# Two transformer blocks on one core: the grouped-query mixer's attention and output projection in another order, and a weight split moved in each FFN

## The reference

```python
def odd_mixer(x, mix_norm, w_qkv, q_norm, k_norm, w_out):
    proj = rms_norm_2(x, mix_norm) @ w_qkv                  # 1024 -> 1536
    q, k, v = jnp.split(proj, [GQA_Q_WIDTH, GQA_Q_WIDTH + GQA_KV_WIDTH], axis=-1)
    q = rms_norm_2(q.reshape(Bsz, S, 16, 64), q_norm)       # 16 heads
    k = rms_norm_2(k.reshape(Bsz, S, 4, 64), k_norm)        # 4 key/value heads
    q, k = apply_rope(q, cos, sin), apply_rope(k, cos, sin)
    return gqa_block_attention(q, k, v) @ w_out             # softmax over 256 keys

def swiglu_ffn_2(x, norm_g, w13, w2):
    g, u = jnp.split(rms_norm_2(x, norm_g) @ w13, 2, axis=-1)
    return (jax.nn.silu(g) * u) @ w2
...
x = x + odd_mixer(...)
x = x + swiglu_ffn_2(...)
```

## Time and profile before

| | |
|---|---|
| median of 3 runs | 1721.07 us (1718.12 to 1721.99) |
| the profiled execution | 1720.91 us |
| its span in the trace | 1719.6 us |
| mean granted TensorE clock | 0.982 |
| TensorE busy | 1641.7 us, 95% of the span |
| VectorE busy | 974.2 us, 57% |
| ScalarE busy | 786.2 us, 46% |
| the odd stage, first projection matmul to first gate matmul of f | 1407.0 to 1528.5 us |

### The profile page before, as it was taken

The page is one execution under the profiler, slowest core; times in us unless marked ns, Lnnn a source line. Parts: engine busy times, 40 slices in busy tenths (PEclk is TensorE's granted clock), DMA queues, the critical chain, the costliest instruction groups (busy, mean ns, idle before and its releaser), DMA issues. The chain is left out here.

```text
span 1719.6 us, 18632 instructions
## 1 busy us (share of the span) xinstructions
PE 1641.7 (95%) x7938; PEld 1343.2 (78%) x7938; DVE 974.2 (57%) x992; ACT 786.2 (46%) x954; POOL 68.4 (4%) x99
## 2 busy tenths in 40 slices
PE   6999998999999999998999999998999997699999
PEld 5877876788888888797788879876788885488887
DVE  4655675545455545645645466877554467545543
ACT  4535444444444443544544446745434345534341
POOL 1000000100000000100100010100000012000000
PEclk9999998999999999999999999999999999799999
DMA  8545542355545554541654544424545443035451
GB/s 328 194 160 185 188 154 85 126 223 190 193 172 202 192 190 177 202 184 57 237 186 181 196 160 195 148 88 109 208 172 196 171 175 147 1 125 218 172 196 50
DMA packets 51391, 289.33 MB, mean 168 GB/s; under 512 B 14151, under 2 KB 14791, under 8 KB 18026
## 3 DMA queue, kind: packets, MB, share of 16 engines
q1 hardware_dynamic: 50732, 286.84, 45.8%
q10 hardware_dynamic: 576, 1.29, 0.2%
HBM read 287.06 MB, written 1.05 MB: 168 GB/s over the span
## 5 line engine op out<-in xcount | busy, mean ns | idle before, releaser
L1764 DVE TENSOR_TENSOR wl<-raw,wh 128x2048 fp32r<-128x2048 f32 x260 | 588.9, 2287 | 156.3 <-ACT wh L1150 156.3
L516 PE MATMUL ps<-wh,xTh 128*128 128x512 f32 x1408 | 558.1, 396 | 20.3 <-DVE wl L1764 8.3
L516 PE MATMUL ps<-wh,xTl 128*128 128x512 f32 x1408 | 552.0, 392 | 0.0
L516 PE MATMUL ps<-wl,xTh 128*128 128x512 f32 x1408 | 551.3, 392 | 0.0
L1150 ACT ACTIVATE wh<-raw 128x2048 fp32r<-128x2048 f32 x260 | 488.9, 1908 | 3.8 <-PE ps L516 2.6
L516 PEld LDWEIGHTS ps<-wh,xTh 128*128 128x128 f32 x1408 | 266.3, 189 | 85.3 <-DVE xTl L1803 10.6
L516 PEld LDWEIGHTS ps<-wh,xTl 128*128 128x128 f32 x1408 | 266.0, 189 | 56.6
L516 PEld LDWEIGHTS ps<-wl,xTh 128*128 128x128 f32 x1408 | 266.4, 189 | 53.7
L2456 POOL TENSOR_SCALAR st<-st 128x1 f32<-128x1 f32 (+2 forms) x46 | 29.5, 640 | 1463.2 <-ACT tmp L1169 850.6
L1213 ACT ACTIVATE sgf<-ps,st 128x256 f32<-128x256 f32 x22 | 10.5, 476 | 104.2 <-PE ps L516 104.2
L1213 ACT ACTIVATE sge<-ps,st 128x256 f32<-128x256 f32 x22 | 10.5, 476 | 98.9 <-PE ps L516 98.9
(11 more groups left out here) (330 smaller groups left out, 2260.8 us busy)
## 6 DMA issues: line engine op xcount, KB each, us to landing
raw<-in_w SPq DMA_DIRECT2D x260, 1024.0 KB, 4.8
gains<-in_rows SPq DMA_DIRECT2D x18, 512.0 KB, 4.1
x<-in_x ACTq DMA_DIRECT2D x2, 512.0 KB, 8.6
nab<-in_rpb SPq DMA_DIRECT2D x32, 32.0 KB, 2.6
out_x<-x SPq DMA_DIRECT2D x2, 512.0 KB, 2.6
qn<-in_rpb SPq DMA_DIRECT2D x16, 32.0 KB, 2.5
xd<-in_rpb SPq DMA_DIRECT2D x16, 32.0 KB, 2.5
df<-in_cst SPq DMA_DIRECT2D x1, 368.0 KB, 23.4
```

Of the source, the lines that this page charges most:

```text
L516: return pe.matmul(o, lhs, rhs, start=start, stop=stop, skip_group_check=False)
L1764: TT(wl[:, p % RAW, :], raw[:, p % RAW, :], wh[:, p % RING, :].bitcast(F32), ALU.subtract).then_inc(*lo(p))
```

## The change

It has two parts.

**1. The odd stage is written in another order**, with its own programs on TensorE, ScalarE and VectorE in place of the shared `attention` and `close`.

- TensorE: q's second half is done in quarters of 6 matmuls (`q_quarter(t, n)`), put between the first scores and turns. From pair 2 on, `out(i, t)`, 6 matmuls of the output projection for one pair and tile, stand between a pair's attention steps: per iteration `scores(i + 1)`, `out(i - 3, 1)`, `values(i - 1)`, `turn(i, 0)`, `out(i - 2, 0)`, `turn(i, 1)`. Both turns of a pair use bank 6 (pair 7: banks 4 and 5), values bank 7, all scores banks 4 and 5. f's tile 0 is turned between the two halves of the very last `out(7, 1)`, with 3 matmuls behind it.
- q is no longer scaled by its norm. VectorE rotates it straight from PSUM; the squares go to a tile of their own (`qsq`); GpSimd writes the roots to a table (`gqa_root`), ScalarE's exponential takes them as its scale, and VectorE multiplies the negated maxima by them (one 128 x 2 multiplication a head). The four 128 x 512 scalings of q are gone.
- ScalarE and VectorE handle a pair head by head, not tile by tile. A dummy exponential at the stage's start loads the table there.
- ScalarE and VectorE copy the turned tile 1 earlier in their programs: VectorE ahead of the tables of gains and of all work on k, ScalarE ahead of `vg`. The splits of the stage's later pieces are spread one an iteration, ahead of the exponentials on ScalarE.

**2. `ring.fill(1, p0)` ahead of the turned input is taken away in every FFN**, on ScalarE and on VectorE. Where that call had split a piece, the next `ring.fill` now does.

No matmul, transpose, exponential or weight piece is added or taken away, and the arithmetic is the same but for the place of q's norm.

```diff
@@ tensor_program, odd @@
-                kv_part(0)
-                q_part(0, 0, 5, lambda: turn_in("oddmix", 1))
-                kv_part(1)
-                q_part(0, 1, 1)
-                q_part(1, 0, 4, lambda: [kv_turn(t) for t in range(2)])
-                for t in range(2):
-                    q_turn(0, t)
...
-                attention("gqa", "odd", 8, 64, [256, 256], q_of, k_of, v_of,
-                          {0: lambda: q_part(1, 1, 7), 3: lambda: [q_turn(1, t) for t in range(2)]})
-                close("odd", "ogqa", 8, None)
+                kv_part(0)
+                q_part(0, lambda: turn_in("oddmix", 1))
+                kv_part(1)
+                q_part(1)
+                q_quarter(0, 0)
+                q_quarter(0, 1)
+                kv_turn(0)
+                kv_turn(1)
+                q_turn(0, 0)
+                q_turn(0, 1)
+                q_quarter(0, 2)
+                scores(0)
...
+                for i in range(3, 7):
+                    scores(i + 1)
+                    out(i - 3, 1)
+                    values(i - 1)
+                    turn(i, 0)
+                    out(i - 2, 0)
+                    turn(i, 1)
...
+                out(6, 1)
+                out(7, 1, lambda: turn_in(AFTER["odd"], 0))
@@ scalar_program and vector_program, ffn @@
                 gate(0, 0)
-                ring.fill(1, p0)
                 ring.need(p0 + 4)
                 turn_in(name, 1, free=free)
@@ scalar_program, odd @@
+                turn(2, 0)
+                ring.fill(1, p0 + 3)
+                for i in range(3, 7):
+                    turn(i - 1, 1)
+                    ring.fill(1, p0 + i + 1)
+                    scores(i + 1)
+                    values(i - 1)
+                    turn(i, 0)
@@ vector_program, odd @@
+                def scores(i):
+                    on.wait_ge(scored, "gqa", i)
+                    for hh in range(2):
+                        a = 12 * (i % 3) + 6 * hh
+                        dve.tensor_reduce(r.sm[:, a:a + 2], bank(4 + hh).rearrange("p (t n) -> p t n", t=2), AX.X, ALU.max, negate=True).then_inc(*made("peak", i, hh))
...
+                        TT(r.sm[:, a:a + 2], r.sm[:, a:a + 2], gqa_root(2 * i + hh), ALU.mult).then_inc(*peaked("gqa", i, hh))
...
+                scores(3)
+                ring.fill(1, p0 + 3)
+                values(1)
+                for i in range(3, 7):
+                    scale(i)
+                    scores(i + 1)
+                    ring.fill(1, p0 + i + 1)
+                    values(i - 1)
```

More of the change, by code:

```diff
@@ new lines, in out @@
+                def out(i, t, mid=None):
+                    p, k = p0 + 6 + i // 2, i % 2
+                    on.wait_ge(act_lo, "ogqa", i)
+                    on.wait_ge(*split_of(p))
+                    if i == 0:
+                        clear(2 * t, 2 * t + 1)
+                    H, L = hi_part(p, 2), lo_part(p, 2)
+                    for half in range(2):
+                        if half and mid:
+                            mid()
+                        u = slice(512 * half, 512 * half + 512)
+                        m = mm3(bank(2 * t + half), xTh[:, i, t, :], xTl[:, i, t, :], H[:, k, u], L[:, k, u], i == 0, i == 7)
+                    if t == 1 and k == 1:
+                        m.then_inc(*multiplied(p))
+                    elif i == 7:
+                        m.then_inc(*tail("odd"))
+                    if i == 7:
+                        emptied[2 * t] = emptied[2 * t + 1] = [post_step("odd", t)]
@@ L1726, in odd @@
-                ring.fill(1, p0 + 4)
+                q_stat(0, 1)
+                v_copy(1)
                 ring.need(p0 + 6)
-                for t in range(2):
-                    on.wait_ge(flipped, "kg", t)
-                    act.activation(od.kTg[:, :, 128 * t:128 * t + 128], halves(6 + t), ACT.Copy).then_inc(*copied("kTg", t))
-                q_stat(1, 0, 4)
-                for t in range(2):
-                    q_turn(0, t)
-                def q_turns():
-                    for t in range(2):
-                        q_turn(1, t)
@@ L1739, in odd @@
-                attention("gqa", "odd", 8, 64, [256, 256], xTh, (multiplied, p0 + 5), lambda i: p0 + (6 if i else 4),
-                          {1: lambda: q_stat(1, 1, 7), 3: q_turns})
-                close("odd")
+                k_copy(0)
+                k_copy(1)
+                q_turn(0, 0)
+                q_turn(0, 1)
+                ring.fill(1, p0 + 2)
+                scores(0)
+                q_stat(1, 0)
+                scores(1)
+                turn(0, 0)
+                q_stat(1, 1)
@@ new lines, in odd @@
+                turn(0, 1)
+                turn(1, 0)
+                scores(2)
+                q_turn(1, 0)
+                values(0)
+                turn(1, 1)
+                scores(3)
+                q_turn(1, 1)
+                values(1)
+                turn(2, 0)
+                ring.fill(1, p0 + 3)
[5 more added lines that the diff above has]
+                    turn(i, 0)
@@ L1743, in scalar_program @@
+                turn(6, 1)
+                ring.fill(1, p0 + 8)
+                values(6)
+                turn(7, 0)
+                turn(7, 1)
+                values(7)
+                seam("odd", 0, p0 + 8)
+                turn_in(AFTER["odd"], 0, free=(tail, "odd"))
+                ring.fill(1, p0 + 9)
+                seam("odd", 1, p0 + 10)
             norm_stat("pre00", None, 0)
@@ L2433, in odd @@
-                close("odd")
+                k_rope(1)
+                q_rope(0, 1)
+                ring.need(p0 + 6)
+                q_sum(0, 1)
+                scores(0)
+                ring.fill(1, p0 + 2)
+                scale(0)
+                scores(1)
+                q_rope(1, 0)
+                q_sum(1, 0)
+                scale(1)
+                scores(2)
+                q_rope(1, 1)
+                values(0)
+                q_sum(1, 1)
+                scale(2)
+                scores(3)
```

266 lines of the change are left out of this document (197 added, 69 removed).

## The result

The changed kernel takes **1695.12 us** (median of 4 runs, 1693.43 to 1696.34) against 1721.04 before (1718.12 to 1721.99): ratio 0.9851, 95% interval 0.9837 to 0.9864. The forecast was 1693.8. The profiled execution has a span of 1692.1 us against 1719.6, so 27.5 us less; the sum had 27.1. It is the fastest of the four runs; the medians lie 25.9 us apart.

A forecast was written before the change was run, and what follows sets the result against it. TensorE, busy 95% of the span, bounds the kernel; only its idle or low-clock time can go. From 1720.9 us, 24.4 in the odd stage and 2.7 at FFN entries leave 1693.8, range 1690 to 1698 (8 in 10: 1687 to 1703).

The forecast's parts named there:

- The stage, 97.1 us: Odd mixer, first projection to f's first gate matmul: floor 86.2 plus holes 10.85 us, a gain of 24.4 us.
- The floor, 86.2 us: Odd stage: TensorE's summed work at the high clock, including 2.0 us for some 20 late starts.
- Holes, 10.85 us: Odd stage, TensorE idle time left: before attention 1.3, first pairs 2.8, split of p0+7 5.65, seam into f 1.1 us.
- The split of piece p0+7: Attention loop: the split stalls VectorE about 4.4 us, giving TensorE holes of 2.2, 1.5, 0.4 and 1.55, sum 5.65 us.
- Entry: Odd stage's start: ScalarE copies the turned input without waiting behind vg, so the 3.35 us hole and slow stretch go.
- The exponentials: Attention loop on ScalarE: exponentials with their accumulator read walked 0.45 us apart.
- I put nothing for the clock in the sum: Odd stage: largest hole 2.2 us, no clock fall counted, since it stayed up behind d's 1.82; one fall costs about 1.6.
- Rival 1: Odd stage: the clock swings; one fall gives 1695, one in each of five iterations 1703 us; chance 0.14.
- FFN entries, 2.7 us: Entries of c and d: holes of 0.70 and 1.82 us go, with late starts 0.8 + 1.9.
- rival 2: Attention loop: ScalarE's order binds each iteration, turn(i,1) waiting for a copy behind exponentials; 1698 to 1702 us; chance 0.12.
- Rival 3: Odd stage: fewer waits than walked, p0+7 stall mostly vanishes, half the holes go; 1688 us; chance 0.12.
- Rivals 4 and 5: Odd stage: 4, clock falls at p0+7 stall and stays down, 1736 (0.02); 5, pair chain stays 6.3 us, 1713 (0.02).

The follow-up runs named there:

- old entry: Changed kernel with the odd stage's entry order undone (ScalarE copies vg, VectorE works on k, ahead of the turned input): 1695.99 us.
- reordered run: Changed kernel with ScalarE's p0+7 split, last q_turn and turn(2,0) copy ahead of pair 3's exponentials, and TensorE's out(0,1) ahead of scores(4): 1688.88 us.
- two swaps: Changed kernel with ScalarE's split and copies moved early, f's input turned earlier, and TensorE's scores(4) and scores(5) each behind an output projection: 1687.35 us.
- part 1 alone: Changed kernel with the FFN splits put back ahead of the turned input, so only the odd stage's new order: 1698.40 us.
- repeat: The changed kernel measured once more, unedited: 1695.71 us.
- split early: Changed kernel with ScalarE making piece p0+7's high part ahead of pair 3's exponentials: 1691.05 us.
- seam: Changed kernel with f's input turned ahead of the last six output projection matmuls, not the last three: 1695.17 us.
- plain exponential: Changed kernel without q's norm in the attention: no exponential scale, a same-size VectorE maximum in place of the product: 1693.06 us.

## Why the prediction was right, step by step

The total was met by the mechanism that was forecast. That it was met to about 1 us is partly luck: within the stage two errors of 1.65 us cancelled, and the two costs that the sum left out, the exponential's scale and the clock, went unseen beside them.

- *The stage, 97.1 us.* Measured 98.25, and 97.05 without the falls of the clock (98.33 - 1.28 in the run with the old entry). Right.
- *The floor, 86.2 us.* Too low. In that same run, at full clock, TensorE was busy for 87.85 of the 98.33 us. The same matmuls took 86.94 and 86.89 us in the reordered run and the one with two swaps, also at full clock and with fewer holes. So 0.9 of the 1.65 us comes and goes with the holes; a likely reason is that the last row ahead of a hole counts with its whole length (0.39 us) and not with the distance to the next start (0.23). The other 0.7 I have not traced; the term for late starts (some 20 of 0.1) is the likeliest, since the alternation makes many more changes from one kind of matmul to another.
- *Holes, 10.85 us.* Too high by as much: in that run, without the entry, 9.2 us were idle, 9.05 of them in holes that the timeline marks. (In the changed kernel itself it is 7.8 idle and 90.4 busy, where I had 11 and 86.2, because its slow matmuls fill some of the holes.) Before the attention 0.61 and not 1.3; first pairs 2.1 and not 2.8; seam 0.88 and not 1.1.
- *"The split of piece p0+7", 5.65 us, "my largest single term and the least certain".* Right in size and place (2.32, 1.14, 0.37, 1.90: 5.73; VectorE's stall 4.62 against 4.4), wrong in one cause: 2.32 of it stay when the split comes early and go when the copy does.
- *Entry.* The 3.35 us hole went for the reason given; with the old order it comes back, but at 1.28. The other 2 us match GpSimd's: the operation ahead of k's root took 2.16 us before, 0.19 in the changed kernel and 0.20 in the one with the old order. No run tries that by itself.
- *Steady iterations, 6.1 us.* 1473.53 to 1479.63 from turn to turn: 6.10. No hole there.
- *The exponentials.* Wrong. I walked them 0.45 apart, from rows of an exponential without a scale; with its scale they stand 0.54 apart. "In exchange the four 128x512 scalings of q go (2.7 us of VectorE)" looked only at VectorE, where there was room. On the path of each pair the folding costs: 2.7 us in the stage.
- *"I put nothing for the clock in the sum".* Wrong step, small price. It rested on one row, the 1.82 us hole in d behind which the clock stayed up, and took that to hold for 2.2 us; the holes to come were 2.3 and 1.9. The row does not even hold for itself: with part 1 alone the clock fell behind the same hole in d. One fall was priced at 1.6, as that one cost; two in the stage cost 1.2 net, because a slow stretch fills idle time behind it. Rival 1 came true in its mechanism, twice rather than five times, though the stage's mean clock was 0.97 and not under 0.95, the sign I had given for it. The quoted section of the Trainium skill (TensorE: Matmul & The Clock Gate, "A second HAM failure mode: psum-queue depth-cycling") has the clock swing on small idle times between groups. In this stage the traces do not agree: the iterations with small holes only, from pair 5 on, stayed at 1.00, and each fall stood behind one hole of 1.9 us or more. Outside the stage three executions show a fall with no hole at all (below), so a long hole is not the only cause.
- *FFN entries, 2.7 us.* 1.0 and 2.1, together 3.1. Right. The 0.84 that the first expectation names for c comes out as 0.96 to 1.00 when it is read at the matmuls behind the hole.
- *Rivals 2 and 3.* The hole before turn(3,1) was there once and not in each iteration, against rival 2. Rival 3 (1688) is what the kernel gives once ScalarE's order is mended (1688.9). Rivals 4 and 5 fell: in the changed kernel the clock came back within 4 us each time, and the iterations are 6.1 us with 2.94 us of projection in them.

## What to carry to other kernels

When dense matmuls are put between the steps of a latency chain, count only those that really stand ahead of the chain's last step, and then look at the engine that serves both: a copy that frees TensorE's bank belongs ahead of the exponentials of the next pair, and a weight split ahead of them too. Work folded into an instruction is free only on the engine that it leaves; price it again on the path of the one it enters. With gains of a microsecond, compare the stage between two marks in the trace, and look at the clock in it, before reading the medians. That the clock stayed up behind a hole in one execution does not say that it will in the next.

## What the runs showed of the hardware

- *The clock behind a hole of the same size is not the same each time.* In the odd stage TensorE's clock fell to 0.50 behind the hole of 2.32 or 2.33 us in five profiled executions of six (changed kernel and its repeat, part 1 alone, split early, seam) and stayed at 1.00 in the sixth (old entry). Behind 1.95 it fell (plain exponential). Behind 1.90 or 1.91 it fell in the four executions where it had also fallen behind the hole of 2.3 us, and stayed in the two where it had not (old entry, reordered). Behind 1.76, 1.67 and 1.54 it stayed. With the projection behind the attention it stayed behind 2.77 and fell behind 2.38 and 2.48. In the changed kernel and its repeat it was back at 1.00 within 4 us. At d's entry it stayed behind 1.82 (kernel before) and fell behind 1.83 (part 1 alone). The cleanest pair is one kernel twice, at one place: in the attention between c and d the hole is 2.15 us in the changed kernel and 2.14 in its repeat, and only the repeat's clock falls behind it; the other stays at 1.00 until 790 us (a row and a window of TensorE, changed kernel, then repeat).

```profile
784.89 0.85 PE L784 MATMUL ps<-ident,sca 128*128 128x128 f32 x6 [2.15 <-ACT PTa L1486]
...
785.00:787.00 2.00, 2.00 (x14) 1.00 0.57 242
```

```profile
786.45 0.84 PE L784 MATMUL ps<-ident,sca 128*128 128x128 f32 x6 [2.14 <-ACT PTa L1486]
...
787.00:789.00 2.00, 2.00 (x10) 0.64 0.32 135
```

- *The clock can also fall with no hole ahead of it.* In the convolution, at 251 us, it fell in three executions of fourteen (the repeat, part 1 alone, seam). TensorE had been busy without a break since at least 236 us in all fourteen. Among its matmuls from 243 us on were some of 80 or 32 partitions; whether these have to do with it is not shown. Windows of the repeat:

```profile
248.00:250.00 2.00, 2.00 (x11) 1.00 0.00 0
...
252.00:254.00 2.00, 2.00 (x7) 0.50 0.00 0
```

- *An exponential whose scale is read from a tile is longer*: 563 ns against 475 for 128x256 with the same bias and accumulator, in two runs without the scale.
- *GpSimd beside VectorE.* The small operation ahead of a root took 0.19 us when no subtraction of a split ran beside it, 2.16 before the change, and 2.27 elsewhere in the new trace beside the subtraction of 1422.48 to 1424.77. The 2.16 us also lay beside one, of 1415.61 to 1417.89. I made no run for this alone.
